# Prompt attention of a streaming encoder layer: value products of a step issued at the head of the next one

## The reference, cut to what matters

```python
def stick_breaking_block(q, k, v, q_pos, k_pos):
    z = jnp.einsum('bqhd,bshd->bhqs', q, k).astype(jnp.float32) * SB_SCALE
    valid = k_pos[None, :] < q_pos[:, None]
    log_keep = jnp.where(valid, jax.nn.log_sigmoid(-z), 0.0)
    log_rest = lax.cumsum(log_keep, axis=3, reverse=True) - log_keep
    a = jnp.where(valid, jnp.exp(jax.nn.log_sigmoid(z) + log_rest), 0.0)
    return jnp.einsum('bhqs,bshd->bqhd', a.astype(v.dtype), v)
```

## Time and profile before

| | |
|---|---|
| median of 3 runs | 2222.02 us (2219.86 to 2224.2) |
| the profiled execution's own time | 2226.82 us |
| its span, first to last instruction | 2225.0 us |
| mean granted TensorE clock | 0.954 |
| prompt attention in that execution, first sigmoid to last value product | 442.0 to 689.5 us |

### The profile page before, as it was taken

One profiled execution on the slowest core, in us unless ns is written; L12 is line 12 of the kernel. 1 busy time (PEld: TensorE's weight loads), 2 busy tenths in 40 slices (PEclk: granted clock), 3 DMA queues, 4 the chain that ended last, 5 costly groups with the idle time before them and its releaser, 6 DMA issues.

```text
span 2225.0 us, 32486 instructions
## 1 busy us (share of the span) xinstructions
PE 2007.8 (90%) x13793; PEld 1857.8 (83%) x13793; DVE 893.9 (40%) x1060; ACT 502.8 (23%) x897; POOL 610.9 (27%) x239
## 2 busy tenths in 40 slices
PE   5999999777777499998998999999999999999799
PEld 4989899744444399888897999999999999999577
DVE  5550335465663366666762252222122221215321
ACT  4231132344444222222212031101011010113110
POOL 5213324000000633333420332443234342343100
PEclk9999999878888699999997999999999999999899
DMA  5021211200002400000002111111111111111101
GB/s 167 21 75 58 100 59 68 83 5 1 1 1 79 145 15 25 19 19 20 24 6 87 39 39 38 57 38 56 38 38 57 38 45 49 38 57 43 64 28 39
DMA packets 90877, 104.30 MB, mean 47 GB/s; under 512 B 9492, under 2 KB 74336, under 8 KB 90784
## 3 DMA queue, kind: packets, MB, share of 16 engines
q1 hardware_dynamic: 81440, 89.96, 12.6%
q10 hardware_dynamic: 9344, 12.98, 1.6%
HBM read 85.32 MB, written 17.60 MB: 46 GB/s over the span
## 4 chain that ended last, share of the span: by engine, by line
PE 79%; DVE 7%; ACT 6%; issue 4%; DMA 2%; POOL 2%; SPq 0%; ACTq 0%; DVEq 0%; POOLq 0%
PE psum L1540 44%; PE psum L1512 5%; PE psum L1513 4%; PE psum L1514 4%; PE psum L1815 3%; PE psum L1819 3%; PE psum L1586 2%; PE psum L1612 2%; PE psum L1804 2%; PE psum L1589 1%; ACT area L922 1%; ACT area L903 1%; DVE area L1164 1%; ACT area L902 1%; PE psum L1738 1%
## 5 line engine op out<-in xcount | busy, mean ns | idle before, releaser
L673 POOL TENSOR_TENSOR w_hi<-w_raw,ones 128x2048 fp32r<-128x2048 f32 x51 | 184.9, 3625 | 1148.1 <-PE psum L1540 623.0
L1540 PE MATMUL psum<-act_hi,w_hi 128*128 128x352 f32 x1248 | 270.0, 324 | 0.8 <-ACT area L1043 0.8
L1540 PE MATMUL psum<-act_hi,w_lo 128*128 128x352 f32 x1248 | 268.9, 323 | 0.0
L1540 PE MATMUL psum<-act_lo,w_hi 128*128 128x352 f32 x1248 | 268.6, 323 | 0.0
L674 POOL TENSOR_TENSOR w_lo<-w_raw,w_hi 128x2048 fp32r<-128x2048 f32 x51 | 254.7, 4995 | 4.0
L1512 PE MATMUL psum<-w_hi,act_hi 128*128 128x256 f32 (+1 forms) x720 | 226.5, 315 | 28.2 <-issue 17.2
L1513 PE MATMUL psum<-w_lo,act_hi 128*128 128x256 f32 (+1 forms) x720 | 221.9, 308 | 0.0
L1514 PE MATMUL psum<-w_hi,act_lo 128*128 128x256 f32 (+1 forms) x720 | 220.9, 307 | 0.0
L1394 DVE TENSOR_TENSOR area<-psum,area 128x1056 f32<-128x1056 f32 x72 | 90.5, 1256 | 317.1 <-PE psum L1540 317.1
L1540 PEld LDWEIGHTS psum<-act_hi,w_lo 128*128 128x128 f32 x1248 | 214.2, 188 | 0.0
L1540 PEld LDWEIGHTS psum<-act_hi,w_hi 128*128 128x128 f32 x1248 | 212.4, 189 | 0.9 <-ACT area L1043 0.9
(11 more groups left out here) (263 smaller groups left out, 3016.4 us busy)
## 6 DMA issues: line engine op xcount, KB each, us to landing
w_raw<-in_w_up_dram SPq DMA_DIRECT2D x16, 1024.0 KB, 5.5
w_raw<-in_w_down_dram SPq DMA_DIRECT2D x16, 1024.0 KB, 5.0
w_raw<-in_w_in_dram SPq DMA_DIRECT2D x14, 1024.0 KB, 5.5
area<-in_x_prompt_dram SPq DMA_DIRECT2D x16, 512.0 KB, 4.0
conv_scratch<-area ACTq DMA_DIRECT2D x12, 512.0 KB, 2.6
area<-conv_scratch SPq DMA_DIRECT2D x8, 768.0 KB, 4.5
w_raw<-in_cache_k_dram SPq DMA_DIRECT2D x2, 2048.0 KB, 9.1
area<-in_cache_v_dram SPq DMA_DIRECT2D x2, 2048.0 KB, 8.6
```

The lines of the kernel that those rows point to most:

```text
L673: own.link(pool.tensor_tensor(hi, w_raw[:, slot, :], ones[:, 0:1].to_broadcast([P, BLK]), ALU.mult))
L1540: last = pe.matmul(bank(base + c)[0:rows, 0:CH], w(k), a[:, k, CH * c:CH * (c + 1)], start=(k == 0 and w is lhs_hi and a is hi), stop=(k = ...
```

## The change

In TensorE's loop the value products of the step before are issued first, ahead of the transposes of head 0 and the scores of step + 2. They stood behind both. Nothing else is changed: the other engines' lists, the semaphores, the buffers and the instructions themselves are the same.

```diff
             scores(0)
             scores(1)
             for step in range(len(STEPS)):
+                if step:
+                    values(step - 1)
                 turn_weights(step, 0)
                 if step + 2 < len(STEPS):
                     scores(step + 2)
-                if step:
-                    values(step - 1)
                 turn_weights(step, 1)
             values(len(STEPS) - 1)
```

## The result

The changed kernel takes 2170.01 us (median of 4 runs, 2168.47 to 2171.21), against 2220.94 for the kernel before (4 runs, 2217.74 to 2224.2): a ratio of 0.977, 95% interval 0.9753 to 0.9787. The forecast was 2164 in a range of 2148 to 2197, faster by more than 0.2%. The profiled execution took 2168.47 us, its span 2166.5.

The account below looks back on a forecast made before the run. The bound was a TensorE-ScalarE loop of waits in the prompt attention. Its 247.5 us would become 176.6 at full clock plus 39.9/3 for low clock, 189.9; 57.6 off gives 2169.2 profiled, 2164 as median, range 2148 to 2197.

Parts of the forecast that it names:

- The old loop: Prompt attention: scores, value products and all of ScalarE's copies and sigmoids follow one another, 242.1 plus 5.4 us of hand-offs.
- steps 1 and 2: Attention loop: head 0's copy runs beside the scores; value products and head 0's transposes run beside and outlast head 1's sigmoids.
- S + G0 + C1 + V + T0: New attention loop: scores, head 0's sigmoids, head 1's copy, value products, head 0's transposes; 176.6 us at full clock with hand-offs.
- Step 3: Attention stretch with the clock as mixed as before: new loop 216.5 us, a gain of 31 from the order.
- Step 4: Attention stretch at full clock throughout: the new loop's terms sum to 176.6 us.
- Step 6: TensorE's clock in the attention: shorter stretches without products leave a third of the low-level share, giving 189.9 us.
- The clock rule: Skill's rule that transposes don't count as busy like products: 32 new waits would be pauses, pushing the attention toward 263.1 us.
- Steps 7 and 8: Attention: the wait ahead of the value products adds nothing, at most 11 us; VectorE, 151.0 us busy, does not become the bound.
- The rival of the mixed clock: Attention loop shortens but the low clock follows as often: gain 31 us, time 2191, chance 0.16.
- Step 5: Attention stretch at the low clock throughout: the new loop's terms sum to 263.1 us.
- The slower rival: TensorE's clock falls after each new pause in the attention: 263.1 us, 15.6 more than before, time 2238, chance 0.03.
- the one without gain: Head 0's copy in the attention is held by something other than the value products: time stays 2222, chance 0.02.

Follow-up runs that it names:

- e8: Changed kernel with the scores of step + 2 moved ahead of the transposes of head 0, value products still first: 2192.24 us, ratio 0.9859.
- e2: Changed kernel plus three dummy products of 384 columns in TensorE's wait ahead of the value products of each wide step: 2167.09 us, ratio 0.9756.
- e5: Kernel before, old order, plus two dummy products of 256 columns in each of TensorE's two waits of each wide step: 2193.72 us, ratio 0.9875.
- e6: Changed kernel plus two dummy products of 256 columns in the wait ahead of the value products of each wide step: 2162.98 us, ratio 0.9739.
- e7: Kernel before with only the narrow blocks' value products, those issued in wide steps, moved ahead: 2210.08 us, ratio 0.9946.
- e1: Kernel before, old order, plus three dummy products of 384 columns in each of TensorE's two waits of each wide step: 2220.8 us, ratio 0.999.

## Why the prediction was right, point by point

**The old loop (242.1 plus hand-offs) and steps 1 and 2.** Right. The chain after is the loop S + G0 + C1 + V + T0 that step 2 wrote down, and e8 shows that the part of step 1 on which it rests, the copy beside the scores, is worth about half of the order.

**Step 3, 31 us from the order alone.** Not tested as it stands: no run held both orders at the old mix of clocks. At full clock the sum's own terms give the order 212.7 - 176.6 = 36 (as e2's expectation has it), and e5 against e6 measured 31.3. That this equals step 3's number is partly luck.

**Step 4, the loop at full clock.** Right. The sum of 176.6 is 44.15 for each of four rounds, and the rounds at full clock took 44.59, in the changed kernel as in e6. For the old order 212.7 is 53.2 a round, and e5 took 52.4.

**Step 6, how much the clock costs.** The size came out, the reason did not. The clock's remainder was put at 13.3, and 192.1 less four rounds of 44.59 is 13.7. But only 2.7 of it are the clock in the loop, the one round with the dip. The other 11.0 stand outside the four rounds, at the start, where the loop fills (26.6 us at a clock of 0.64), and at the end. The sum has no term for these: in e5 and e6 as well some 8.5 us lie outside four full-clock rounds. So the remainder that was meant for falls in the loop happened to cover a start that was left out, and 189.9 forecast against 192.1 measured is in that part luck. The share was near in the same way: 0.93 against 0.81 is 14% of the time at the low level against 38%, about a third, but most of it stands ahead of the loop.

**The clock rule.** Step 6 weighed the Trainium skill's "TensorE: Matmul & The Clock Gate", Part 4, that transposes do not count as TensorE being busy in the way that products do. The runs neither show nor refute the sentence itself, but what the prediction took to follow from it here, a pause at each of the 32 new waits and with it the low level, didn't come: between 466.5 and 544.8 and from 551.7 on the granted clock is 1.00, with products in every step and a wait ahead of them of 1.34 us on average. The rows on which step 6 rests were also not all there were. The same view of the kernel before has a stretch of transposes alone that is longer than the 2.94 us of the earlier trace rows and was followed by the full clock:

```profile
554.15:558.27 4.12, 1.47 (x10) 1.05 (x10) 2.52 (x4) 4.03 (x8) 0.00 (x0) 1.00 0.01 2
558.27:562.00 3.73, 3.52 (x39) 2.90 (x40) 3.30 (x6) 1.08 (x4) 0.00 (x0) 1.00 0.00 0
```

So the length of such a stretch did not decide by itself. The changed kernel says the same. The wait ahead of the one dip was of the longest kind (TensorE's rows from 540 us on):

```profile
539.81 0.49 PE L1600 MATMUL psum<-ident,area 128*128 128x128 f32 x3
542.45 1.31 PE L1612 MATMUL psum<-area 128*64 128x128 f32 x20 [2.14 <-ACT area L922]
543.69 0.33 PE L1600 MATMUL psum<-ident,area 128*128 128x128 f32 x1
544.28 1.10 PE L1586 MATMUL psum<-area 64*128 64x256 f32 x4 [0.26 <-ACT area L903]
545.31 1.22 PE L1589 MATMUL psum<-ahead,ident 128*128 128x128 f32 x4
```

Line 1589 takes 1.22 us at 545.31 and 0.71 at full clock. The same wait of 2.14 us, ahead of the same products, stands at 497.86 and at 589.70 too, and no fall followed there. Step 6 counted two steps in a round of eight as near the length that fell; it was one in the four rounds once the loop ran. What decides whether the clock falls stays open.

**Steps 7 and 8.** The wait ahead of the products costs nothing beyond its hand-off of 0.04 in the chain, the lower end. VectorE isn't the bound: its waits for the sigmoids stay (45.3), and the splits' wait fell from 51.4 to 3.7. ScalarE's wait of 29.6 for the transposes was not among the signs named; it costs nothing in the chain.

**Sum and rivals.** The forecast of the profiled execution, 2169.2, met 2168.47, in part by luck: the stretch was 2.2 us longer than forecast, and the rest of the program some 3 us shorter than before, 2.1 of it ahead of the stretch. The medians differ by 50.9, and not by 57.6, since the profiled execution of the kernel before was 5.9 above the median of the four runs (4.8 above that of the three known before), and that of the changed kernel 1.5 below: the 4.8 was taken over to the changed kernel as if it had belonged to every execution. So 2164 was 6 us too low, well inside the range. The rival of the mixed clock would have been 216.5 in the stretch; e7, whose clock stayed at 0.82, shows that half a change can leave the clock as it was. Step 5's sum at the low clock was not run. The slower rival and the one without gain didn't come.

## What to carry to other kernels

When a wait between two engines closes into a loop, write the loop down as a sum and test that it closes before moving anything; then ask of every term whether it needs what stands ahead of it in its queue. Moving the products paid in two ways: a copy on another engine came to run beside the scores, which was about half of the order's worth, and the products came to run beside the last sigmoids. The next term to move, the transposes, could be read from the chain of the changed kernel. A new order can raise the clock of TensorE as well, so its terms are to be taken at both levels. And a loop's sum is best tested on one undisturbed round; the start and the end of the stage need a term of their own.

## What was not expected

In the DeltaNet stage TensorE sometimes stands still with nothing to wait for that the profile shows. The waits of that stage, the kernel before first, then e1:

```profile
PEld psum L1797 <- issue: 3.5, 1, 3.5
```

```profile
PEld psum L1807 <- issue: 9.6, 4, 2.8
```

It is the same place in both (e1 has ten lines more above it), once in the one and four times in the other, and absent from the changed kernel's list. A loop round of this stage of 49.6 us took 54.6 in the kernel before and twice 56.8 in e1. In the changed kernel no round was longer, but from VectorE's last row of line 1251 to the first addition of the stage behind (line 1394) it was 82.7 us instead of 78.3, so the two stages came out nearly equal (470.2 and 469.3) by two differences that cancel. In the profile of e1 the longer rounds took back more than half of what the stretch had gained (16.1). Whether it explains e1's median over 10 runs, and what it waits for, was not tried and stays open. It means that a gain of this size is better read in its own stage than in the total.
